# SyncE's order of DMAs in the gated delta rule of a decoder layer: page pairs before query and gate loads, spill and sample states in six pieces

## The reference

```python
u = rmsnorm(x) @ w_in                          # one projection for all branches
A = conformer_conv(u_a, conv_buf, ...)         # branch A
B = gated_deltanet(u_b, qkv_buf, s0, ...)      # branch B: chunked delta rule, then gated RMSNorm
...
kc, vc, c_end = nsa_compress(full[:, :, 0:2], w_pos)   # branch C: 32-token blocks of the cache, weighted sums
...
def step(S, xs):                               # the delta rule's state step
    v_new = vw_i - einsum('bhck,bhkv->bhcv', kcd_i, S)
    o_i = einsum('bhck,bhkv->bhcv', q_i * exp(g_i)[..., None], S) + einsum('bhij,bhjv->bhiv', qk_i, v_new)
    S = S * exp(g_end)[..., None, None] + einsum('bhck,bhcv->bhkv', k_i * exp(g_end - g_i), v_new)
```

## Time and profile before

| | |
|---|---|
| median of 3 runs | 2857.33 us (2854.47 to 2863.16) |
| the profiled execution's own time | 2862.0 us |
| its span, first to last instruction | 2860.3 us |
| granted TensorE clock over the span | 0.96 |
| TensorE busy | 2664.0 us, 93% of the span |
| POOL, DVE, ACT busy | 24%, 46%, 30% |
| delta rule, tile 0 to the end of tile 7 | about 791 to 1041 us |

### The profile page before, as it was taken

One profiled execution on the slowest core, in us unless ns is written; L12 is line 12 of the kernel. 1 busy time (PEld: TensorE's weight loads), 2 busy tenths in 40 slices (PEclk: granted clock), 3 DMA queues, 4 the chain that ended last, 5 costly groups with the idle time before them and its releaser, 6 DMA issues. The chain is left out here.

```text
span 2860.3 us, 53119 instructions
## 1 busy us (share of the span) xinstructions
PE 2664.0 (93%) x21998; PEld 2443.6 (85%) x21998; DVE 1315.1 (46%) x2314; ACT 854.8 (30%) x1604; POOL 696.8 (24%) x557
## 2 busy tenths in 40 slices
PE   8999999999889887788888999999999999999996
PEld 7999999999867764455558899988999999999996
DVE  5999999213143346455543353224333323324234
ACT  4333111123122324555652222135221121120221
POOL 1222222212143330121203424200422222222233
PEclk9999999999988887999999999999999999999998
DMA  5112352322386725334316552233111111111111
GB/s 178 51 60 60 102 106 85 95 93 76 112 253 200 213 94 204 121 119 150 116 41 219 154 186 62 74 120 147 45 45 45 51 46 45 45 45 45 45 51 61
DMA packets 148834, 290.35 MB, mean 102 GB/s; under 512 B 28100, under 2 KB 96648, under 8 KB 145842
## 3 DMA queue, kind: packets, MB, share of 16 engines
q1 hardware_dynamic: 136930, 255.48, 28.5%
q0 software_dynamic: 11520, 31.47, 3.5%
q10 hardware_dynamic: 144, 0.00, 0.0%
HBM read 245.94 MB, written 51.93 MB: 104 GB/s over the span
## 5 line engine op out<-in xcount | busy, mean ns | idle before, releaser
L165 POOL TENSOR_TENSOR mlp_w_low<-mlp_w_raw,mlp_w_high 128x1024 fp32r<-128x1024 f32 x72 | 174.6, 2425 | 650.8 <-ACT mlp_w_high L161 650.8
L362 PE MATMUL in_psum<-x_high,in_w_high 128*128 128x352 f32 x1416 | 266.3, 330 | 23.8 <-DVE x_low L557 13.8
L165 POOL TENSOR_TENSOR in_w_low<-in_w_raw,in_w_high 128x1024 fp32r<-128x1024 f32 x59 | 145.5, 2466 | 575.5 <-ACT in_w_high L161 575.5
L2769 PE MATMUL mlp_psum<-mlp_in,mlp_w_high 128*128 128x352 f32 x1536 | 264.9, 324 | 0.0
L362 PEld LDWEIGHTS in_psum<-x_high,in_w_high 128*128 128x128 f32 x1416 | 236.2, 190 | 32.3 <-issue 17.0
L161 ACT ACTIVATE mlp_w_high<-mlp_w_raw 128x1024 fp32r<-128x1024 f32 x72 | 76.4, 1061 | 624.2 <-PE mlp_psum L2769 624.2
L362 PE MATMUL in_psum<-x_low,in_w_high 128*128 128x352 f32 x1416 | 260.5, 326 | 0.0
L362 PE MATMUL in_psum<-x_high,in_w_low 128*128 128x352 f32 x1416 | 258.6, 324 | 0.0
L2769 PEld LDWEIGHTS mlp_psum<-mlp_in,mlp_w_high 128*128 128x128 f32 x1536 | 251.2, 189 | 0.2
L362 PEld LDWEIGHTS in_psum<-x_low,in_w_high 128*128 128x128 f32 x1416 | 236.6, 191 | 0.0
L362 PEld LDWEIGHTS in_psum<-x_high,in_w_low 128*128 128x128 f32 x1416 | 234.3, 189 | 0.0
(11 more groups left out here) (473 smaller groups left out, 4473.0 us busy)
## 6 DMA issues: line engine op xcount, KB each, us to landing
mlp_w_raw<-in_w_mlp SPq DMA_DIRECT2D x64, 512.0 KB, 3.6
in_w_raw<-in_w_in SPq DMA_DIRECT2D x59, 512.0 KB, 4.3
nsa_ring<-in_cache_slc SPq DMA_DIRECT2D x144, 128.0 KB, 3.9
u_scratch<-stage SPq DMA_DIRECT2D x32, 528.0 KB, 5.3
gdnp_page_ring<-in_cache_cmp POOLq DMA_DIRECT2D x128, 128.0 KB, 4.7
gdnp_page_ring<-in_cache_cmp SPq DMA_DIRECT2D x128, 128.0 KB, 4.3
nsa_ring<-in_cache_slc POOLq DMA_DIRECT2D x112, 128.0 KB, 4.0
aux<-u_scratch SPq DMA_DIRECT2D x24, 528.0 KB, 3.9
```

The source lines that it names most:

```text
L165: self.nc.gpsimd.tensor_tensor(self.low[:, i % 2, 0:k * P], self.raw[:, i % 2, 0:k * P], self.high[:, i % 2, 0:k * P].bitcast(F32), ALU.su ...
L362: return mm(psum[:, e % 2, n, 0:WN], w[:, i % 2, c * P:(c + 1) * P], a[:, c, n * WN:(n + 1) * WN], start=x == 0 and c == 0, stop=x == 2 an ...
L2769: return mm(psum[:, e % 2, n, 0:WN], w[:, i % 2, c * P:(c + 1) * P], a(c)[:, column(n)], start=x == 0 and c == 0, stop=x == 2 and c == CHU ...
```

## The change

In SP's list the spill goes out in two pieces of 1056 KB and the sample states come in four pieces of 512 KB. The new function `load_late(k)` issues piece k, one at the end of each loop t = 1 to 6. Inside the loop, `load(t + 2)` moves behind the third page step, `load_gate(t + 1)` behind the fifth. Semaphore counts follow. Bytes, and the work of every other engine, stay the same.

```diff
@@ SP, before the loop
-            sp.dma_start(spill, conv).then_inc(sent, 16)
             sp.dma_start(own[:, :], t_dram["sample_own"]).then_inc(own_in, 16)
-            sp.dma_start(state_s[:, :, :, :], t_dram["state_gdn"]).then_inc(state_in, 16)
+
+            def load_late(k):
+                if k < 2:
+                    sp.dma_start(spill[:, 2 * k:2 * k + 2, :], conv[:, 2 * k:2 * k + 2, :]).then_inc(sent, 16)
+                else:
+                    b = 2 * (k - 2)
+                    sp.dma_start(state_s[:, b:b + 2, :, :], t_dram["state_gdn"][:, b:b + 2, :, :]).then_inc(state_in, 16)
+
@@ SP, the loop
             for t in range(NT):
-                if t + 2 < NT:
-                    load(t + 2)
-                for step in range(t * STEPS + RING, min((t + 1) * STEPS + RING, NB * STEPS)):
+                for k, step in enumerate(range(t * STEPS + RING, min((t + 1) * STEPS + RING, NB * STEPS))):
                     load_pages(sp, step, (0, 1), pages_in)
                     if step % 2:
                         spread_bias(step // 2 - RING // 2)
-                if t + 1 < NT:
-                    load_gate(t + 1)
+                    if k == STEPS - RING and t + 2 < NT:
+                        load(t + 2)
+                    if k == STEPS - RING + 2 and t + 1 < NT:
+                        load_gate(t + 1)
+                    if k == STEPS - 1 and 1 <= t < 7:
+                        load_late(t - 1)
                 if t == NT - 3:
-                    sp.wait_ge(sent, 16)
+                    sp.wait_ge(sent, 32)
@@ the end of SP's list, and TensorE's sample_values
-            sp.wait_ge(sent, 16 * (2 + H))
+            sp.wait_ge(sent, 16 * (3 + H))
-                pe.wait_ge(state_in, 16)
+                pe.wait_ge(state_in, 16 * 4)
```

## The result

The changed kernel takes 2868.68 us (median of 8 runs, 2864.51 to 2878.08), the kernel before 2859.15 us beside it (8 runs, 2854.47 to 2863.62). The ratio of the runs is 1.0038 with a 95% interval from 1.0026 to 1.0050; between the two medians lie 9.5 us, 0.33%. The forecast was 2855 us with a range from 2838 to 2866; the time lies above both.

What follows compares the result with a forecast made beforehand. The two DMA engines carrying the bias copies were taken as the bound. 10.5 us of lead, less 11.3 of moved work, plus 3 of idle time, gave 2.2 us off 2857.3: 2855 us, range 2838 to 2866.

Steps and rivals of the forecast that it cites:

- What bounds the kernel: Delta rule, loop 0 to compress 6 of tile 6: the two DMA engines carrying the bias copies are the bound.
- The 31.0 us a tile: Estimated work per tile of the two bias-copy DMA engines, against 28.0 us that TensorE needs.
- The first rival: Pages are late through SP's order and the new order mends it: 18 us gain, 2835 to 2848 us, chance 0.28.
- Lead of 10.5 us: Loop's first pages issued near 801 us instead of 811.75, as spill and states leave the list before the loop.
- C66: Start of compress 6 of tile 6 on TensorE, forecast 2.2 us earlier; sign: within 7 us of 1005.87.
- 11.3 us of moved work: Spill, states and tile 2's query load put back on the bias-copy engines ahead of tile 6's compress 6 pages.
- The states' share: Three states pieces of 1.25 us, issued before the pages of compress 6 of tile 6: 3.75 us.
- The spill's 5.1 us: Time of the spill on the bias-copy engines, put back in two pieces behind tiles 1 and 2.
- the query load's 2.4 us: Tile 2's query load, formerly before the loop's first pages, now after them: 2.4 us on the bias-copy engines.
- 3 us of idle time regained: Reordering in the loop removes idle time of the bias-copy engines: taken as 3 us, bounds 0 and 6.5.
- The second rival: The lead is lost as SP waits for ring places in tiles 0 and 1: 2861 to 2869 us, chance 0.15.
- the forecast's own signs: First pages near 801 us; tiles 0 to 3 near 28 to 30 us without page wait; tiles 5 and 6 longer.

Runs made afterwards that it cites:

- experiment 4: Kernel before, each bias copy made as two, one a head, with 16 column blocks outermost to use 16 DMA engines: 2844.03 us, ratio 0.9956.
- experiment 2: Kernel before with only the query and gate loads moved inside the loop, spill and states left ahead of it: 2860.87 us, ratio 1.0004.
- experiment 1: Changed kernel with the gate load put back at the loop's end: 2862.44 us, ratio 1.0015 against the kernel before.
- experiment 6: Changed kernel, order kept, with three places for z instead of two: 2866.79 us, ratio 1.0023 against the kernel before.
- experiment 9: Changed kernel with the gate load at the loop's end and the four states pieces behind the last pages: 2861.42 us, ratio 1.0007.
- experiment 3: Kernel before with only spill and states moved, as six late pieces, no reordering in the loop: 2862.50 us, ratio 1.0012.
- experiment 8: Changed kernel with the gate load at the loop's end and bias copies on 16 DMA engines: 2849.12 us, ratio 0.9959.
- experiment 5: Changed kernel with each bias copy made as two that run on 16 DMA engines: 2849.63 us, ratio 0.9964 against the kernel before.

## Why the prediction was wrong

**What bounds the kernel: right.** The pair of engines that carries the bias copies was the bound. Spreading those copies took away every page wait and 0.44% of the time. The 31.0 us a tile were an estimate from rows; experiment 4 tests that the pair bounds the stage, and not that number. The Trainium skill, "DMA: Bandwidth & Descriptors", section "Why a DMA increments its semaphore by 16 and not by 1", has the number of engines follow the slowest dimension, as the largest number up to 16 that divides it, and always the lowest-numbered ones. By that, 16 blocks outermost should spread a copy over all 16, and experiment 4 agrees (share 0.54 in place of 0.13 at the end of the stage); that two engines are the lowest-numbered ones no run here shows. The first rival, that the order is to blame, falls with experiment 2: the order alone gives 1.0004.

**Lead of 10.5 us: there, and then lost.** The first pages went out 10.95 us earlier, tiles 0 and 1 took 30.12 and 28.39 us, and tile 2 began with a lead. Then the step failed that reads "for compress 6 of tile t that takes 2.4 us of query load off the pair (the gate is still in front, two steps earlier in the loop before)": it counted the gate's transfer, and nothing for its wait. (The gate load moved up by three page steps, from behind the eighth to behind the fifth, and not by two.) The gate load carries a wait for POOL (`gated` of t - 1). At the loop's end that wait is 0.2 us long (experiment 1); three page steps earlier it holds SP 8.7 us in loop 1 and 3.6 in loop 6, with the pages of three steps, two bias copies and the late piece queued behind it in the list that feeds the pair with all but POOL's pages. Removing the wait with the order kept (experiment 6) or moving the load back (experiment 1) gives C66 7.4 us back; so of the 10.4 us lost at C66, 7.4 are this. In time it is 0.0023 of the ratio by experiment 1 and 0.0015 by experiment 6, with intervals that touch or overlap. The wait in loop 6 cannot be part of it, since it ends at 1022.67, behind C66; what it delays has cover, as compress 6 of tile 7 follows C66 after 31.4 us (1047.62) and before after 32.3 (1038.16).

**11.3 us of moved work: right in kind.** The states' share was tested alone: 3.75 us by the sum, 3.4 measured (experiment 9). The spill's 5.1 us and the query load's 2.4 us were not.

**3 us of idle time regained: none.** This was a middle value between 0 and 6.5; experiment 2, which has the new order alone, shows no gain, and C66 4.1 us late. With it at 0, the sum is 11.3 - 10.5 = 0.8 us late, where experiments 1 and 6 show 2.9 and 3.0. The table of page issues says where 0.8 us more may lie: in experiment 1 the lead is 7.6 us by tile 1, and 9.7 at the fourth page step of loop 1 (840.25 against 849.95), not 10.5; 11.3 - 9.7 = 1.6 us. The last 1.3 us stay open. What the profile of one execution can tell is not much finer: two profiles of the changed kernel differ by 0.2 us at C66 and by 6.2 us in the span.

**The sum again.** At C66 the way from the changed kernel to the one before goes by experiments 1 and 9: 7.4 us for the gate wait, 3.4 for the states in front, and -0.5 for the rest. That these add up to the 10.4 us in the trace is so by construction and proves nothing; what each step is, the experiments say.

**Tile 6, which the account leaves open.** Starts on TensorE, and the time between them, in us:

| kernel | compress 6 of tile 5 | C66 | between |
|---|---|---|---|
| before | 972.25 | 1005.87 | 33.6 |
| after | 974.03 | 1016.26 | 42.2 |
| experiment 1 | 969.70 | 1008.81 | 39.1 |
| experiment 2 | 971.10 | 1009.98 | 38.9 |
| experiment 3 | 971.81 | 1009.17 | 37.4 |
| experiment 6 | 969.45 | 1008.88 | 39.4 |
| experiment 9 | 968.49 | 1005.39 | 36.9 |

By tile 5 the gate wait has cost 4.3 us (974.03 against 969.70); the rest of the 7.4 comes in tile 6. And each of these changed kernels loses 3.3 us or more there against the kernel before, experiment 2 too, which has no late piece and by then no gate wait. What they have in common was not isolated, and the kernel before was profiled only once.

**The rivals.** The second rival gave 2861 to 2869 us and a start of compress 6 of tile 6 after 1012 us, and both came; its mechanism only in small part, so that its numbers were right mostly by luck. SP's waits for places of the ring are 2.8 us in two places, and experiment 1, without the loss, has 2.1. The lead was lost to a wait that no rival named, though its line stood in the part of the code that the diff moves. I had given this side 0.15, and slower 0.11; the reason against it, that the pair has a backlog as soon as bias copies run, does not hold over a stop of 8.7 us. Of the forecast's own signs the first pages came at 800.80 us as said, but tile 3 took 33.56 us where 28 to 30 were forecast, and C66 was 10.4 us late where 7 were allowed.

## What to carry to other kernels

Before a DMA is moved up in an in-order list, read the wait in front of it and look up in the trace when its releaser runs: the gate ran at 854.61 us, SP arrived at 847.2, and everything behind it in the list was held. Ask also what stands ahead of the releaser in its own engine's list; here it was six page issues that it did not need. A lead that is lost on the resource that bounds the stage shows as lateness many tiles later (C66 is 7.4 us later with the stop of loop 1 than without), so look for the first stretch in which that resource runs dry rather than at the longest wait. And where a few DMA engines carry most of the work, mend the shape of the copy first: that was worth 0.44%, and every reordering of the list between nothing and a loss.

## What the runs showed that was not expected

With the pair's bound gone, the lead brought nothing. Experiment 8 reaches tile 1 at 816.47 us, 6.6 us before experiment 4 (823.12), and C66 at the same time (993.98 and 993.95). TensorE waits for no page in either. Its granted clock in tiles 1 to 5 is 0.94, 0.88, 0.89, 0.94, 0.89 there, and 0.91, 0.94, 0.94, 0.94, 1.00 in experiment 4 (means over the two levels, 1.2 and 2.4 GHz): in the mean the kernel that ran ahead was granted less. That goes with the loss of the lead only over the whole stretch: tile 3 has the lower clock in experiment 8 and is shorter (28.38 against 30.17 us), and tile 1 has the higher one and is longer (29.62 against 28.85). What made the lead go was not tried.

A wait of SP and its cost are far apart: 30.5 us at the gate load cost experiment 5 too little against experiment 4 to be told in time (0.9964 against 0.9956, overlapping intervals) and 3.4 us at C66, and one stop of 8.7 us cost the changed kernel 7.4 us there. Nor is the loop's end free of such waits: in experiments 4 and 8, which leave the gate load there, SP waits at it 6.2 and 7.1 us in four places each.
